# A transformer layer on one core: where a mixer slot puts its attention work, and which engine normalises group A's outputs

## The chip, the cores and the metric

One core of a Trainium2 chip runs one program. The metric is the device time of one execution in microseconds, median of three runs. The engines are named as in the profile: PE (TensorE, matmuls and transposes), PEld (its weight loads), DVE (VectorE), ACT (ScalarE), POOL (GpSimd), SP (SyncE, which only issues DMAs). Each runs its own list of instructions in order and waits on semaphores that the others raise.

## The reference

One layer of an encoder, for 512 prompt positions and, with a past of 512, for 32 sample positions. What matters here:

```
mod = silu(c) @ w_mod + b_mod             # shift, scale, gate for both sub-layers
h   = RMSNorm(x) * (1 + scale_a) + shift_a
z   = h @ w_in                            # q, k, v of groups A and B
A (8 heads, 128 wide): two softmax maps over two halves of q and k,
    w = p0 - lambda * p1;  o = w @ v
    o = RMSNorm(o over the 128) * g * (1 - lambda_init)      # g = subln_g, one value per column
B (16 heads, 64 wide): softmax with a sink over a window, o = p @ v
x = x + gate_a * (concat(A, B) @ w_out)
x = x + gate_f * (silu(conv(h2 @ w_up)) gated @ w_down)      # then a last RMSNorm
```

The normalisation of A multiplies each row (a position) by one number, 1/rms, and each column by one number, g. Once the 128 x 128 result is turned, a column of it is a partition.

## The kernel before

Positions stand on the free axis of the transposed activations: T = 544 columns in two halves of 272, D = 2048 in 16 k-tiles of 128. All large products are made of three matmuls per k-tile, high x high, low part of x, low part of w (`products`, L1590 to L1592). A weight chunk of 128 x 1024 is loaded by SP into one of four raw buffers, ACT copies its high part (w_hi, L829), DVE subtracts for the low part (w_lo, L1188).

**Half-steps and slots.** The projection z is computed slab by slab: 36 slabs of 128 columns, each in two half-steps (hf), 72 in all; one half-step takes 16 k-tiles, 48 matmuls. The attention is cut into points, `TURNS`: for each A head i = 0 to 3 for the four prompt blocks of 128 queries, i = 4 and 5 for the two softmax maps of the sample; for each B head pair four. The points of A head h are worked on in half-steps 6(h+1) to 6(h+1)+5, one to a half-step, while PE makes the slabs of the next head; so group A fills half-steps 6 to 53. B's points share half-steps in twos. `make_slots` gives the list of slots (half-step, part, parts, point t, item), and each engine's block walks that list in its own written order; nothing is planned at run time. In slot k, `pt` is the point of slot k-1 and `pp` that of slot k-2, where they have an output (i = 4 of A has none).

**A point's way.** Its score is made at the end of the slot before its own (`score`, L1645, into a PSUM bank). DVE adds the bias and takes the maximum (`softmax_max`, L1307, L1314), ACT the exponential with row sums (`softmax_exp`, L899), DVE joins the two maps (`combine`, L1334 to L1338). One slot later PE turns the probabilities (`turn_probs`, L1663, into bank 6), ACT (for A) or DVE (for B) copies them to SBUF (L919 to L922), PE multiplies by the values (`values`, L1679, into bank 7). For A, ACT then scales the result by 1/sum (o_raw, L951) and sums its squares (L952), POOL makes 1/rms in two small steps (`rstd`, L710, L711), and DVE multiplies o_raw by 1/rms and by g (o_norm, L1379; g was broadcast to all partitions, 128 x 128). Another slot later PE turns o_norm (`turn_output`, L1688) and ACT copies it into oT (L928).

**Beside it.** During half-steps 2 to 49 the parts of `mod` that are wanted later are computed off PE: SP loads 80 chunks of w_mod (L512), between the chunks of w_in (L520) and into the same four buffers. Half of each chunk's sum is made on DVE (`late_sum`, L1276, L1279), the other half as products on ACT (`late_mul`, L888) and sums on POOL (`late_add`, L725). `late_of` gives a slot's chunks: `begin` and `end`, one or none each, 1.67 per half-step on average. A raw buffer is free when DVE's w_lo has read it, or, for a chunk of w_mod, when DVE's late sum and ACT's late product have (`slot_free`, L489 to L493); SP issues strictly in stream order.

**The order around the change.** PE in a slot: quarter of the half-step's products, turn of the probabilities (pt), quarter, turn of the output (pp), quarter, values (pt), score of the next point, a turn of k or v (item), last quarter (`products_between`). ACT: exp (t), copy of the probabilities, copy of the output (pp), w_hi of the chunk two half-steps on, `late_mul` of begin, o_raw and square (pt), item, `late_mul` of end. DVE: z out of PSUM (L1289), copies for B, w_lo, combine (t), maximum of the next point, `late_sum` of begin, o_norm (pt), `late_sum` of end. POOL: `late_add` of begin, rstd (pt), table of the next head's bias, stores and loads of k and v, `late_add` of end. In the six slots of the tail (half-step None) PE puts the first tiles of the output projection in place of the products.

Of the kernel before, what the change touches and what calls it, by code (L numbers as in the profile page):

```python
# [33 lines left out]
ALU = mybir.AluOpType  # L34
ACT = mybir.ActivationFunctionType

P = 128
# [74 lines left out]
def is_a(t):  # L112
    return TURNS[t][0] < A_HEADS


def has_out(t):
    return not (is_a(t) and TURNS[t][1] == 4)
# [27 lines left out]
TAIL = len(SLOTS) - 6  # L145
# [58 lines left out]
def scored_ahead(t):  # L204

    return is_a(t) or TURNS[t][1] > 0
# [8 lines left out]
def prev_out(k, back):  # L215

    t = SLOTS[k - back][3] if k >= back else None
    return t if t is not None and has_out(t) else None
# [22 lines left out]
def late_of(hf, part, parts):  # L241

    if hf is None:
        return [], []
    c = [n for n, h in enumerate(LATE_AT) if h == hf]
    if parts == 1:
        return c[:1], c[1:]
    return (c[:1] if part == 0 else c[1:] if part == 1 else []), []
# [56 lines left out]
def build(nc, A, O):  # L305
# [5 lines left out]
    with ctx:  # L311
        def on(stack, name, shape, dt=F32):
            return stack.enter_context(nc.sbuf_tensor(name, shape, dt))
# [54 lines left out]
        tab_a = on(st1, "tab_a", [P, TAB])  # L368
        tab_b = on(st1, "tab_b", [P, 256])
        tab = [on(st1, f"tab{i}", [P, TAB]) for i in range(2)]  # L370
        gsub = on(st1, "gsub", [P, P])
        st1.close()

        st2 = ExitStack()
# [202 lines left out]
        def _(pool):  # L577
# [89 lines left out]
            for x in "kv":  # L667
# [4 lines left out]
            pool.wait_ge(scratch_out, 16 * 4)  # L672
            load_past("k", 0)
            load_past("v", 0)
            pool.dma_start(gsub[:, :], A["subln_g"].partition_broadcast(P).rearrange("p a n -> p (a n)")
                           ).then_inc(ld_sub, 16)

            step(pool.iota(tab_a[:, :], pattern=[[1, TAB]], base=-512, channel_multiplier=-1,
                           allow_small_or_imprecise_dtypes=True))
# [53 lines left out]
            for k, (hf, part, parts, t, item) in enumerate(SLOTS):  # L733
                pt = prev_out(k, 1)
                begin, end = late_of(hf, part, parts)
                for n in begin:
                    late_add(n)
                if pt is not None and is_a(pt):
                    rstd(pt)
                if t is not None and TURNS[t][1] == 0 and next_table < 16:  # L740
                    table(next_table)
                    next_table += 1
                if item:
                    natural(*item)
                    if item[1] == "p" and next_pk < 10:
                        load_past("k", next_pk)
                        next_pk += 1
                if pt is not None and TURNS[pt][1] == (5 if is_a(pt) else 3):
                    last_of_kv = pt + 1 == len(TURNS) or kv_of(TURNS[pt + 1][0]) != kv_of(TURNS[pt][0])
                    if last_of_kv and next_pv < 10:  # L750
                        pool.wait_ge(t_pv, OUT_COUNT[pt])
                        load_past("v", next_pv)
                        next_pv += 1
                for n in end:
                    late_add(n)
# [42 lines left out]
        def _(act):  # L798
# [111 lines left out]
            h_hi(KT - 1)  # L910
            for k, (hf, part, parts, t, item) in enumerate(SLOTS):
                pt, pp = prev_out(k, 1), prev_out(k, 2)
                if t is not None and scored_ahead(t):
                    softmax_exp(t)
                if pt is not None and is_a(pt):
                    act.wait_ge(b6_done, USE6[("p", pt)])
                    if pv_blocks(pt)[0][0] == P:
                        n = P * len(pv_blocks(pt)[0][3])
                        act.activation(probsT[:, 0:n], B6[:, 0:n], ACT.Copy).then_inc(b6_free, 1)  # L919
                    else:  # L920
                        act.activation(probsT[:, 0:P], B6[:, 0:P], ACT.Copy)
                        act.activation(probsT[0:TS, P:P + TS], B6[0:TS, P:P + TS], ACT.Copy).then_inc(b6_free, 1)  # L922
                if pp is not None:
                    act.wait_ge(t_ot, OUT_COUNT[pp])
                    if TURNS[pp][0] >= KT - 8:
                        act.wait_ge(m_late, LATE1 // LPG * LGT)
                    for n, c, tok, _b in pv_blocks(pp):
                        ins = act.activation(oT[:, TURNS[pp][0], tok:tok + n],  # L928
                                             B7[:, 256 + c:256 + c + n], ACT.Copy)
                    ins.then_inc(t_otev, 1)  # L930
                if t is not None and not scored_ahead(t):
                    softmax_exp(t)
                if hf is not None and part == 0 and hf + 2 < FC0:
                    hi_early(hf + 2)
                begin, end = late_of(hf, part, parts)
                for n in begin:
                    late_mul(n)
# [188 lines left out]
        def _(dve):  # L1126
# [214 lines left out]
            for k, (hf, part, parts, t, item) in enumerate(SLOTS):  # L1341
                pt = prev_out(k, 1)
                if (hf and part == 0) or k == TAIL:
                    z_out(hf - 1 if hf else ZH - 1)
                if hf == 5:
                    dve.wait_ge(ld_sub, 16)
                    dve.tensor_scalar(gsub[:, :], gsub[:, :], 1.0 - LAMBDA_INIT, None, ALU.mult).then_inc(small_ok, 1)
                    dve.wait_ge(small_ok, 1)
                if t is not None and not scored_ahead(t):
                    softmax_max(t)  # L1350
                if pt is not None and not is_a(pt):
                    dve.wait_ge(b6_done, USE6[("p", pt)])
                    if TURNS[pt][1] < 3:
                        dve.tensor_copy(probsT[:, :], B6[:, :]).then_inc(b6_free, 1)
                    else:
                        dve.tensor_copy(probsT[:, 0:2 * P], B6[:, 0:2 * P])
                        for e in range(2):
                            c = 256 + 64 * e
                            dve.tensor_copy(probsT[:, c:c + TS], B6[:, c:c + TS])
                            ins = dve.tensor_copy(probsT[0:TS, c + TS:c + 2 * TS], B6[0:TS, c + TS:c + 2 * TS])  # L1360
                        ins.then_inc(b6_free, 1)
                if hf is not None and part == 0 and hf + 2 < FC0:
                    lo_early(hf + 2)
                if hf is None:
                    for kt in TAIL_SPLITS[k - TAIL]:
                        dve.wait_ge(n_hi, KT + kt + 1)
                        dve.tensor_tensor(x_lo[:, kt, :], oT[:, kt, :], x_hi[:, kt, :].bitcast(F32), ALU.subtract
                                          ).then_inc(x_ok, 1)
                if t is not None and has_out(t):
                    combine(t)  # L1370
                if next_ahead(k) is not None:
                    softmax_max(next_ahead(k))
                begin, end = late_of(hf, part, parts)
                for n in begin:
                    late_sum(n)
                if pt is not None and is_a(pt):
                    dve.wait_ge(t_rstd, OUT_A[pt])
                    n = pv_blocks(pt)[0][0]
                    dve.scalar_tensor_tensor(out=o_norm[0:n, 0:P], in0=o_raw[0:n, :], scalar=stats[0:n, pt % 4, 19:20],  # L1379
                                             in1=gsub[0:n, :], op0=ALU.mult, op1=ALU.mult).then_inc(t_on_a, 1)  # L1380
                for n in end:
                    late_sum(n)

            def gated(n, h, b, gate):

# [139 lines left out]
        def _(pe):  # L1525
# [183 lines left out]
            for k, (hf, part, parts, t, item) in enumerate(SLOTS):  # L1709
                pt, pp = prev_out(k, 1), prev_out(k, 2)  # L1710
                n = KT // parts
                cut = [n * part + n * c // 4 for c in range(5)]

                def products_between(c):


                    if hf is not None:
                        tiles(hf, range(cut[c], cut[c + 1]))
                    elif k > TAIL and c in (1, 2):
                        tiles(ZH + c - 1, TAIL_SPLITS[k - TAIL - 1])  # L1720

                if t is not None and not scored_ahead(t):
                    score(t)
                products_between(0)
                if pt is not None:
                    turn_probs(pt)
                products_between(1)
                if pp is not None:
                    turn_output(pp)
                products_between(2)  # L1730
                if pt is not None:
                    values(pt)
                if next_ahead(k) is not None:
                    score(next_ahead(k))
                if item:
                    kv_item(*item)
                products_between(3)
            tiles(ZH, TAIL_SPLITS[-1])
            tiles(ZH + 1, TAIL_SPLITS[-1])
            for hf in range(ZH + 2, ZH + OH):  # L1740
# [118 lines left out]
```

## Time and profile before

| | us |
|---|---|
| median of 3 runs (lowest, highest) | 2827.66 (2827.05, 2828.97) |
| the profiled execution | 2829.49 |
| its span in the profile | 2827.7 |
| PE busy in it | 2620.3 (93%) |
| DVE, ACT, POOL busy | 1658.2, 994.1, 638.3 |

A stretch of the span is read with the busy time of each engine in it and with the clock that was granted to PE, as a share of 2.4 GHz. A wait is idle time of an engine right before an instruction, put down to what was signalled last. The mixer's half-steps run from about 182 us to 950 us of the span; the stretch 231 to 734 holds half-steps 6 to 53.

### The profile page before, as it was taken

To read this page: it belongs to the slowest core of one execution; us is meant where nothing else is said; L and a number is where in the kernel's file an instruction comes from. 1 tells how busy PE (TensorE), PEld (TensorE's weight loads), DVE (VectorE), ACT (ScalarE), POOL (GpSimd) and SP (SyncE) were. 2 spreads that over 40 slices of the span, in tenths; PEclk is the share of its full clock that TensorE was granted. 3 is DMA by queue.
4 is the path that set the end of the run, shared out by engine and by line. 5 is a ranking of instruction groups with operands and counts; after the bars stand their busy time and mean duration, and the time that the engine had idled before them with its cause. 6 is when DMAs were issued, how large, how long until landed. Compare 5 with 4: busy or idle time off the path is not lost.

```text
span 2827.7 us, 50285 instructions
## 1 busy us (share of the span) xinstructions
PE 2620.3 (93%) x19815; PEld 2469.0 (87%) x19815; DVE 1658.2 (59%) x2930; ACT 994.1 (35%) x1975; POOL 638.3 (23%) x534
## 2 busy tenths in 40 slices
PE   6688888888999999789999999999999999999997
PEld 2267777777898899689999999999999999999997
DVE  6878777776445788785444444444444444444454
ACT  5555554554434433542222222222222222222224
POOL 4776566665100344331000000000000000000003
PEclk9889999999999999899999999999999999999998
DMA  9764444445221556253233333223333222322231
GB/s 299 229 196 147 157 137 155 148 146 144 61 63 47 154 165 174 74 157 110 83 89 90 91 90 90 87 80 90 90 90 91 86 83 87 91 85 84 87 105 67
DMA packets 416207, 325.00 MB, mean 115 GB/s; under 512 B 44394, under 2 KB 360202, under 8 KB 414880
## 3 DMA queue, kind: packets, MB, share of 16 engines
q1 hardware_dynamic: 410032, 302.55, 35.9%
q0 software_dynamic: 5248, 14.63, 1.6%
q10 hardware_dynamic: 688, 4.47, 0.4%
q8 instruction: 169, 2.77, 0.4%
q14 instruction: 70, 0.57, 0.1%
HBM read 307.73 MB, written 14.07 MB: 114 GB/s over the span
## 4 chain that ended last, share of the span: by engine, by line
PE 55%; DVE 5%; DMA 2%; issue 2%; ACT 1%; SPq 1%; ACTq 0%; POOL 0%; DVEq 0%
PE ps L1592 18%; PE ps L1590 18%; PE ps L1591 18%; DVE late_f L1279 3%; DMA w_raw<-in_w_out 2%; ACT w_hi L829 1%; SPq L538 1%; DVE w_lo L1188 0%; DVE x L1387 0%; DVE x_lo L1180 0%; ACT x_hi L1022 0%; DVE cv L1173 0%; PE ps L1809 0%; DVE late_f L1276 0%; DMA w_raw<-in_w_up 0%
## 5 line engine op out<-in xcount | busy, mean ns | idle before, releaser
L1590 PE MATMUL ps<-x_hi,w_hi 128*128 128x272 f32 x4480 | 1328.2, 296 | 44.7 <-DVE w_lo L1188 26.0
L1592 PE MATMUL ps<-x_hi,w_lo 128*128 128x272 f32 x4480 | 1308.2, 292 | 0.0
L1591 PE MATMUL ps<-x_lo,w_hi 128*128 128x272 f32 x4480 | 1298.0, 290 | 0.0
L1590 PEld LDWEIGHTS ps<-x_hi,w_hi 128*128 128x128 f32 x4480 | 855.1, 191 | 62.4 <-issue 23.8
L1591 PEld LDWEIGHTS ps<-x_lo,w_hi 128*128 128x128 f32 x4480 | 856.4, 191 | 0.0
L1592 PEld LDWEIGHTS ps<-x_hi,w_lo 128*128 128x128 f32 x4480 | 853.6, 191 | 0.0
L1188 DVE TENSOR_TENSOR w_lo<-w_raw,w_hi 128x1024 fp32r<-128x1024 f32 x432 | 536.5, 1270 | 463.8 <-ACT w_hi L829 462.7
L829 ACT ACTIVATE w_hi<-w_raw 128x1024 fp32r<-128x1024 f32 x432 | 442.0, 1056 | 837.2 <-PE ps L1592 545.3
L1591 PE MATMUL ps<-y_lo,w_hi 128*128 128x272 f32 x1408 | 407.3, 289 | 0.0
L1590 PE MATMUL ps<-y_hi,w_hi 128*128 128x272 f32 x1408 | 405.7, 288 | 0.0
L1592 PE MATMUL ps<-y_hi,w_lo 128*128 128x272 f32 x1408 | 405.0, 288 | 0.0
L784 POOL TENSOR_TENSOR ext<-cv 128x544 f32<-128x544 f32 x1 | 1.5, 1512 | 1473.4 <-ACT cv L1085 1473.4
L1590 PEld LDWEIGHTS ps<-y_hi,w_hi 128*128 128x128 f32 x1408 | 265.5, 189 | 0.1
L1592 PEld LDWEIGHTS ps<-y_hi,w_lo 128*128 128x128 f32 x1408 | 264.8, 188 | 0.0
L1591 PEld LDWEIGHTS ps<-y_lo,w_hi 128*128 128x128 f32 x1408 | 264.6, 188 | 0.0
L1387 DVE SCALAR_TENSOR_TENSOR x<-ps,mod,x 128x272 f32<-128x272 f32 (+2 forms) x576 | 207.8, 400 | 95.6 <-PE ps L1592 95.5
L1035 ACT ACTIVATE ext<-ps 128x272 f32<-128x272 f32 (+2 forms) x264 | 73.9, 317 | 528.5 <-PE ps L1592 528.0
L725 POOL TENSOR_TENSOR oT<-oT 128x512 f32<-128x512 f32 x150 | 216.3, 1442 | 180.3 <-ACT oT L888 169.5
L1431 DVE COPY ext<-cols 128x2 f32 (+1 forms) x88 | 14.9, 169 | 400.8 <-ACT ext L1035 400.8
L725 POOL TENSOR_TENSOR late_f<-late_f 128x512 f32<-128x512 f32 x90 | 138.4, 1537 | 146.6 <-ACT late_f L888 137.8
L1279 DVE SCALAR_TENSOR_TENSOR oT<-w_raw,cs,oT 128x512 f32<-128x512 f32 x150 | 162.8, 1085 | 3.7
L1279 DVE SCALAR_TENSOR_TENSOR late_f<-w_raw,cs,late_f 128x512 f32<-128x512 f32 x90 | 129.4, 1437 | 3.1
(200 smaller groups left out, 2221.8 us busy)
## 6 DMA issues: line engine op xcount, KB each, us to landing
w_raw<-in_w_mod SPq DMA_DIRECT2D x192, 512.0 KB, 4.7
w_raw<-in_w_up SPq DMA_DIRECT2D x176, 512.0 KB, 4.7
w_raw<-in_w_down SPq DMA_DIRECT2D x88, 512.0 KB, 4.4
w_raw<-in_w_in SPq DMA_DIRECT2D x56, 512.0 KB, 3.9
w_raw<-in_w_in SPq DMA_DIRECT2D x32, 256.0 KB, 3.7
w_raw<-in_w_out SPq DMA_DIRECT2D x16, 512.0 KB, 5.3
w_raw<-in_w_out SPq DMA_DIRECT2D x64, 128.0 KB, 3.9
x_transposed<-xT SPq DMA_DIRECT2D x4, 1088.0 KB, 5.7
```

What stands on the lines that cost most here:

```text
L538: sp.dma_start(dst[64 * u:64 * u + 64, 4 * m:4 * m + 4, :], src.rearrange("(i p) n -> p i n", p=64)).then_inc(ld_raw[slot], 16)
L725: ins = pool.tensor_tensor(acc, late_prod(n, 0) if p == 0 and k == 1 else acc, late_prod(n, k), ALU.add)
L784: pool.tensor_tensor(f_sum, f_sq[0][:, 0:T], f_sq[1][:, 0:T], ALU.add).then_inc(f_add, 1)
L829: act.activation(w_hi[c % NW][:, :], w_raw[raw][:, :], ACT.Copy).then_inc(s_hi, 1)
L1035: ins = act.activation(ext[x][:, a + 2 + 2 * g:a + 2 + 2 * g + n], bank(2 * x + h)[:, a - HALF[h][0]:a - HALF[h][0] + n], ACT.Copy)
L1188: dve.tensor_tensor(w_lo[c % NW][:, :], w_raw[raw][:, :], w_hi[c % NW][:, :].bitcast(F32), ALU.subtract).then_inc(s_lo, 1)
L1279: ins = dve.scalar_tensor_tensor(out=acc_d(g), in0=w, scalar=c, in1=acc_d(g), op0=ALU.mult, op1=ALU.add)
L1387: ins = dve.scalar_tensor_tensor(out=x1[:, n, a:a + m], in0=b[:, a - HALF[h][0]:a - HALF[h][0] + m], scalar=mod[:, gate + n, g:g + 1], in1 ...
L1431: dve.tensor_copy(ext[x][:, TP + 2:TP + 4], cols[:, STATE:STATE + 2, bass.ds(tile, 1)] .rearrange("p a b -> p (a b)")).then_inc(ext_ok, 1)
L1590: pe.matmul(out[:, 0:n], hi_w, hi_x, start=first, stop=False)
L1591: pe.matmul(out[:, 0:n], hi_w, lo_x, start=False, stop=False)
L1592: return pe.matmul(out[:, 0:n], lo_w, hi_x, start=False, stop=last)
```

## The change

PE has two attention points in a slot: products (5 of 16 k-tiles), then the turns of the probabilities (pt) and of the output (pp) together, products (7), then values, score and item, products (4). A's o_norm is made by ACT with 1/rms alone, at the head of its next slot; g is one column, loaded as such, and goes in as the scale of ACT's copy of the turned output. ACT's w_hi now stands ahead of that copy. On DVE the first late sum goes to the head of the slot, combine ahead of w_lo, the maximum of the next point to the end. On POOL rstd goes ahead of the first late add.

```diff
-        gsub = on(st1, "gsub", [P, P])
+        gsub = on(st1, "gsub", [P, 1])
# POOL
-            pool.dma_start(gsub[:, :], A["subln_g"].partition_broadcast(P).rearrange("p a n -> p (a n)")
-                           ).then_inc(ld_sub, 16)
+            pool.dma_start(gsub[:, :], A["subln_g"].rearrange("a p -> p a")).then_inc(ld_sub, 16)
...
+                if pt is not None and is_a(pt):
+                    rstd(pt)
                 for n in begin:
                     late_add(n)
-                if pt is not None and is_a(pt):
-                    rstd(pt)
# ACT
                 pt, pp = prev_out(k, 1), prev_out(k, 2)
+                if pp is not None and is_a(pp):
+                    act.wait_ge(t_rstd, OUT_A[pp])
+                    n = pv_blocks(pp)[0][0]
+                    act.activation(o_norm[0:n, 0:P], o_raw[0:n, :], ACT.Copy, scale=stats[0:n, pp % 4, 19:20]
+                                   ).then_inc(t_on_a, 1)
                 if t is not None and scored_ahead(t):
                     softmax_exp(t)
...
+                if hf is not None and part == 0 and hf + 2 < FC0:
+                    hi_early(hf + 2)
                 if pp is not None:
                     act.wait_ge(t_ot, OUT_COUNT[pp])
...
+                    if is_a(pp):
+                        act.wait_ge(small_ok, 1)
                     for n, c, tok, _b in pv_blocks(pp):
-                        ins = act.activation(oT[:, TURNS[pp][0], tok:tok + n],
-                                             B7[:, 256 + c:256 + c + n], ACT.Copy)
+                        ins = act.activation(oT[:, TURNS[pp][0], tok:tok + n], B7[:, 256 + c:256 + c + n], ACT.Copy,
+                                             scale=gsub[:, 0:1] if is_a(pp) else 1.0)
                     ins.then_inc(t_otev, 1)
                 if t is not None and not scored_ahead(t):
                     softmax_exp(t)
-                if hf is not None and part == 0 and hf + 2 < FC0:
-                    hi_early(hf + 2)
# DVE
+                begin, end = late_of(hf, part, parts)
+                for n in begin:
+                    late_sum(n)
                 if pt is not None and not is_a(pt):
...
+                if t is not None and has_out(t):
+                    combine(t)
                 if hf is not None and part == 0 and hf + 2 < FC0:
                     lo_early(hf + 2)
...
-                if t is not None and has_out(t):
-                    combine(t)
+                for n in end:
+                    late_sum(n)
                 if next_ahead(k) is not None:
                     softmax_max(next_ahead(k))
-                begin, end = late_of(hf, part, parts)
-                for n in begin:
-                    late_sum(n)
-                if pt is not None and is_a(pt):
-                    dve.wait_ge(t_rstd, OUT_A[pt])
-                    n = pv_blocks(pt)[0][0]
-                    dve.scalar_tensor_tensor(out=o_norm[0:n, 0:P], in0=o_raw[0:n, :], scalar=stats[0:n, pt % 4, 19:20],
-                                             in1=gsub[0:n, :], op0=ALU.mult, op1=ALU.mult).then_inc(t_on_a, 1)
-                for n in end:
-                    late_sum(n)
# PE
-                cut = [n * part + n * c // 4 for c in range(5)]
+                cut = [n * part + n * c // 12 for c in (0, 4, 9, 12)]
...
-                    elif k > TAIL and c in (1, 2):
+                    elif k > TAIL and c:
                         tiles(ZH + c - 1, TAIL_SPLITS[k - TAIL - 1])
...
                 products_between(0)
                 if pt is not None:
                     turn_probs(pt)
-                products_between(1)
                 if pp is not None:
                     turn_output(pp)
-                products_between(2)
+                products_between(1)
                 if pt is not None:
                     values(pt)
...
-                products_between(3)
+                products_between(2)
```

## Rows read from the trace of the kernel before

**Rows 1.** Stretches: us, busy (instructions) of PE, PEld, DVE, ACT, POOL; PEclk, DMA, GB/s.
```profile
231.00:734.00 503.00, 435.86 (x3102) 386.51 (x3101) 369.87 (x683) 250.44 (x595) 291.60 (x271) 0.95 0.46 143
734.00:905.00 171.00, 166.97 (x1325) 150.79 (x1325) 79.51 (x303) 69.02 (x241) 16.41 (x23) 1.00 0.22 56
905.00:950.00 45.00, 39.95 (x294) 34.66 (x293) 28.44 (x90) 27.50 (x83) 4.83 (x6) 0.92 0.25 81
```

**Rows 2.** Waits from 231 to 734: who for whom, us in total, times, longest.
```profile
DVE w_lo L1188 <- ACT w_hi L829: 99.1, 43, 5.2
...
PE ps L1688 <- DVE o_norm L1379: 53.7, 30, 3.0
...
PE ps L1663 <- DVE scores L1338: 11.8, 10, 2.9
```

**Rows 3.** Waits of SP's DMA queue from 231 to 734.
```profile
SPq L520 <- DVE oT L1279: 178.9, 41, 6.8
```

**Rows 4.** Timeline 512.2 to 526.5, one slot: start, us, engine, what, idle before.
```profile
512.35 0.83 PE L1679 MATMUL ps<-v_nat,probsT 128*128 128x128 f32 x6
...
513.42 1.06 ACT L829 ACTIVATE w_hi<-w_raw 128x1024 fp32r<-128x1024 f32 x1 [2.10 <-DMA w_raw<-in_w_in]
...
515.61 0.34 ACT L951 ACTIVATE o_raw<-ps,stats 128x128 f32<-128x128 f32 x1
...
515.78 2.99 POOL L725 TENSOR_TENSOR oT<-oT 128x512 f32<-128x512 f32 x2 [5.32 <-ACT oT L888]
...
516.11 0.19 ACT L952 ACTIVATION_READ_ACCUMULATOR square<-ps,stats 128x1 f32 x1
...
516.68 1.33 ACT L888 ACTIVATE oT<-w_raw,cs 128x512 f32<-128x512 f32 x2
...
517.67 0.65 PE L1663 MATMUL ps<-ident,scores 128*128 128x128 f32 x4
...
518.58 1.54 DVE L1279 SCALAR_TENSOR_TENSOR oT<-w_raw,cs,oT 128x512 f32<-128x512 f32 x2
...
518.85 0.53 POOL L710 TENSOR_SCALAR stats<-stats 128x1 f32<-128x1 f32 x1
...
519.04 0.29 PE L1591 MATMUL ps<-x_lo,w_hi 128*128 128x272 f32 x1
...
519.41 0.28 PE L1591 MATMUL ps<-x_lo,w_hi 128*128 128x272 f32 x1
...
519.47 1.08 POOL L711 TENSOR_TENSOR stats<-stats,tiny 128x1 f32<-128x1 f32 x1
...
520.15 0.37 SPq L520 DMA_DIRECT2D w_raw<-in_w_in  x1
520.50 0.84 POOL L650 DMA_DIRECT2D out_ak_p<-k_nat  x1
...
520.58 2.22 DVE L1379 SCALAR_TENSOR_TENSOR o_norm<-o_raw,stats,gsub 128x128 f32<-128x128 f32 x1 [0.46 <-POOL stats L711]
...
522.85 0.40 PE L1688 MATMUL ps<-ident,o_norm 128*128 128x128 f32 x1 [3.03 <-DVE o_norm L1379]
...
523.28 0.43 PE L1591 MATMUL ps<-x_lo,w_hi 128*128 128x272 f32 x1
...
523.96 0.43 PE L1591 MATMUL ps<-x_lo,w_hi 128*128 128x272 f32 x1
...
524.38 1.06 ACT L829 ACTIVATE w_hi<-w_raw 128x1024 fp32r<-128x1024 f32 x1 [0.82 <-DMA w_raw<-in_w_in]
```

**Rows 5.** Groups by shape from 231 to 734: busy us, mean ns, idle before.
```profile
L1379 DVE SCALAR_TENSOR_TENSOR o_norm<-o_raw,stats,gsub 128x128 f32<-128x128 f32 x32 | 26.5, 828 | 7.9 <-POOL stats L711 7.9
...
L725 POOL TENSOR_TENSOR oT<-oT 128x512 f32<-128x512 f32 x134 | 191.2, 1427 | 171.7 <-ACT oT L888 162.0 <-issue 2.3 <-POOL oT L725 0.3
...
L696 POOL TENSOR_SCALAR tab<-tab_a 128x640 f32<-128x640 f32 x6 | 13.1, 2180 | 0.3
...
L928 ACT ACTIVATE oT<-ps 128x128 f32<-128x128 f32 x32 | 8.9, 277 | 82.1 <-PE ps L1688 82.1
```

More of the change, by code:

```diff
@@ L1347, in _ @@
                     dve.tensor_scalar(gsub[:, :], gsub[:, :], 1.0 - LAMBDA_INIT, None, ALU.mult).then_inc(small_ok, 1)
-                    dve.wait_ge(small_ok, 1)
                 if t is not None and not scored_ahead(t):
                     softmax_max(t)
+                begin, end = late_of(hf, part, parts)
+                for n in begin:
+                    late_sum(n)
                 if pt is not None and not is_a(pt):
```

## The prediction, made before the changed kernel was run

> **What bounds the kernel now.** I read the stretches first, then the waits of PE inside one stretch, then SP's waits, then one slot in order of time, and last the groups with their means.
>
> The stretches [rows 1] cut the mixer in three. While group B's points run (734 to 905) PE is busy 166.97 of 171.00 us at clock 1.00: nothing is to be had there. While group A's points run (231 to 734, half-steps 6 to 53, so 48 slots of 10.5 us) PE is busy 435.86 of 503.00 us, so 67 us idle, and its mean granted clock is 0.95. The tail (905 to 950) has 5 us of idle time.
>
> The waits of that stretch [rows 2] say what the 67 us are: 53.7 us are the turn of the output (L1688) behind DVE's o_norm, 30 times, up to 3.0 us; 11.8 us are the turn of the probabilities (L1663) behind DVE's combine. That is 65.5 of 67.
>
> Why o_norm is late can be read in one slot [rows 4]. PE ends the values of a point at 513.18 (512.35 + 0.83). ACT reads them only at 515.61, because it stands in its order behind w_hi, whose chunk landed at 513.42, and a mod product. Pool then takes its late add (515.78, 2.99 us) before the two small rstd steps (518.85 to 520.55). DVE does o_norm from 520.58, for 2.22 us, and PE, which had nothing left since 519.82 (3.03 before), turns the output at 522.85. From the end of the values to the turn: 9.7 us. The chunk of 513.42 was itself late: SP's longest wait of this kind [rows 3] is the issue of w_in behind DVE's late sum, 178.9 us in 41 times, and in rows 4 a late sum of 518.58 to 520.12 is followed by the issue at 520.15. So DVE's old order closes a ring: late sum, load, w_hi, w_lo, combine, max, late sum. That ring is also behind the 99.1 us for which DVE's w_lo waits for w_hi [rows 2].
>
> The stall has a second price, the clock. One k-tile of products (three matmuls) goes from 519.04 to 519.41, 0.37 us, ahead of the stall, and from 523.28 to 523.96, 0.68 us, right behind it [rows 4]: the lower of the two levels, 1.2 instead of 2.4 GHz. A mean of 0.95 over 503 us means 50 us at the lower level. There PE does 0.37/0.68 = 0.54 of its work, a loss of 23 us if it was busy throughout; it was busy for 87% (435.86/503), so 20 us.
>
> **The change part by part.**
>
> *The normalisation.* DVE loses 32 operations of 828 ns and 8 smaller ones, some 30 us of its 369.87 [rows 5, 1]. ACT gets 40 activations of 128x128 from SBUF with a scale from memory. None such is in the trace. The nearest below is the copy of the output, 0.28 us with a constant scale [rows 5]; above it the 128x512 products, 0.67 each (1.33 for two, 516.68 in rows 4). I take o_raw's 0.34 us (515.61), which has the same size and the same kind of scale: 14 us on an engine busy for 250 of 503 [rows 1], 11 to 27 by the two ends. The same o_norm on DVE took 2.22 us in rows 4 and 0.83 in the mean. The Trainium skill (SBUF — State Buffer, "Who interferes with whom") says that a VectorE instruction with two SBUF inputs contends with a GpSimd one that reads SBUF, while ScalarE never waits for anyone; the trace agrees on the DVE side, and by the rule ACT's price would stay at its lowest.
>
> *Pool's order.* rstd now goes before the slot's late add: the 2.99 us between 515.78 and 518.85 leave the path. The price: the late add waits for o_raw, which in rows 4 would move it by 0.5 + 1.7 us. ACT's next product but one waits for it, a slot later, so this hides under a slot.
>
> *DVE's order.* The first late sum goes to the head of the slot, before combine and w_lo. It needs only its own chunk, which was issued a slot earlier, so the ring above opens: the next w_in chunk no longer hangs on combine and max. What then releases it is ACT's mod product in the middle of the slot; a load takes 4.2 us (issued 520.15, w_hi at 524.38) and so ends near the start of the next slot, where w_hi wants it some 3 us in. Were it late still, w_hi's wait would stay: rival B. combine comes out ahead of w_lo and needs only ACT's exp; its reader on PE is five k-tiles into the next slot. I cost the 11.8 us of L1663 as gone.
>
> *PE's two points.* Of 16 k-tiles, 5, 7 and 4 stand before the turns, between turns and values, and after the score (before: 4, 4, 4, 4). Between the values and the turn of that point's output stood 12 k-tiles, now 9: 9 x 0.37 = 3.3 us, with the turn of the probabilities (0.65) 4.0 us, score and kv item not counted. The new chain in that time: o_raw to the end of the square's sum 0.7 us (515.61 to 516.30), rstd 1.7, o_norm 0.34: 2.8 us; ACT's own queue behind o_raw ends at 518.01, 2.4 us after o_raw began, as rstd would. Slack 1.2 us. The added wait stands at the head of ACT's slot, and exp, the copy of the probabilities, w_hi and the copy of the output stand behind it; all but exp are wanted later than o_norm itself.
>
> *What is late next.* Pool. In the slot that also builds the table (once a head) it has rstd 1.7, two late adds of two 1.427 us steps (5.7), the table 2.18 and two DMA issues of 0.84: 11.3 us [rows 4, 5], where the slot should now be (503 - 85.5)/48 = 8.7 us. It falls 2.6 us behind; 1.2 of that is slack, the other 1.4 reach PE, with a little left for the slot after: I take 1.6 us a head, 13 us for eight. Bounds: 0, and 40 turns x 1.0 us.
>
> *Small edits at no price.* g as one column: its load is issued ahead of the first point and waited for once, by DVE in half-step 5 (uncovered, at most the 4.2 us of a whole chunk); on the copy of the output the scale costs at most 0.08 us x 40 on ACT, hidden. w_hi before that copy delays it by 1.06 us at most, and the values that need it stand 7 k-tiles (2.6 us) behind. In B's slots and in the tail the products only change places: PE has no idle time in B, and the tail can give between 4 us gain (of its 5) and 2 us loss (the last turn has nothing in front of it); I take 0.
>
> *Sum.* 53.7 + 11.8 + 20 = 85.5 gained, 13 lost again: 72.5. Against the profiled execution's own 2829.49: 2757. That one lies 1.8 us above the median shown, so against 2827.66: 2755. In sentences of its own: the Trainium skill (TensorE: Matmul & The Clock Gate, "Terms") prices throttled time at that time x (1 - K/N), which for 50 us at half is 25 us where I have 20; by it the sum would be 5 us better, 2750.
>
> **The rivals.**
>
> *A. The wait only changes its releaser.* turn_output now stands before 11 of 16 k-tiles and the values, so ACT behind Pool may be late as DVE was. For it: Pool is busy 291.6 of 503 us, 70% of the shorter stretch, and in order. Against it: 2.8 us of chain in 4.0. Price: half of the 53.7 stays (27) and the clock goes on falling (20): gain 38, 2790.
>
> *B. DVE takes over.* If w_hi goes on landing late, DVE keeps its 99.1 us of waiting beside 340 us of work: 439 us where PE would need 418. The gain is 64, less the 13: 51, 2777. For it: DVE then is at 81% without any wait. Against it: its waits move off the ring.
>
> *C. Slower: a ring through Pool.* Place: rstd behind both late adds of the slot before. Loop: 7 k-tiles 2.6, values 0.83, o_raw and square 0.7, two late adds 5.7, rstd 1.7, o_norm 0.34, turn 0.4 = 12.3 us, against 10.5 now. If it closes in the two of three slots with two mod chunks: 32 x 1.8 = 58 lost, 16 x 1.8 = 29 gained, 2857. It decides from 3.9 us of Pool work in front of rstd in the mean. Against it: Pool's 291.6/48 = 6.1 us a slot.
>
> *D. Nothing to measure*, gains and new waits equal.
>
> **How the numbers follow.** Forecast 0.61 (its own range 2738 to 2772: all of 85.5 and the tail's 4, or twice the new wait and a little), A 0.20, B 0.10, C 0.06, D 0.03. A difference under 0.2% (5.7 us) can't be told from none. Faster 0.91, the same 0.03, slower 0.06. The range goes from 2738 to past A's time, 2795; outside it lie C, D, the worse part of A and a little below.
>
> **What would show it.** Right: between half-steps 6 and 53 PE's waits at the output's turn fall from 53.7 to under 15 us, those at the probabilities' turn to under 3, the mean clock there to 0.99 or more, the stretch shrinks from 503 to about 430 us, DVE's wait for w_hi to under half of 99, B's stretch stays 171. Wrong: PE's turn waits for ACT's o_norm over 25 us and that for Pool's rstd (A, C); or PE idles behind DVE's combine or zq, with w_hi still behind its load (B).

## The result, and the profile after

The changed kernel takes 2740.2 us (2738.19 to 2740.53) where the kernel before, on the same chip, takes 2828.31: a ratio of 0.9679 (95% interval 0.9665 to 0.9694), which on the 2827.66 us shown ahead is 2736.9 us, 91 us less. Measured once more among the experiments the ratio was 0.9711 (0.9698 to 0.9724), 82 us less. So the change is faster, by more than the 72.5 us of the sum, and the first measurement lies just past the fast end of the range. Differences below some 0.3% between separate measurements are therefore read from stretches of the traces here, not from times.

The stretches of the changed kernel, cut where DVE takes half-steps 0, 6, 53 and 71 out of PSUM (columns as in rows 1), and then the same first two stretches of the kernel before. The second of them is called the middle stretch from here on.

```profile
183.40:227.10 43.70, 42.17 (x333) 41.13 (x331) 39.29 (x46) 19.21 (x29) 37.41 (x26) 1.00 0.65 193
227.10:638.20 411.10, 404.53 (x3061) 366.71 (x3061) 350.50 (x631) 262.80 (x628) 295.13 (x272) 1.00 0.58 173
638.20:824.50 186.30, 182.56 (x1451) 164.68 (x1450) 86.35 (x332) 78.21 (x270) 17.30 (x25) 1.00 0.21 54
```
```profile
182.20:231.40 49.20, 45.80 (x346) 44.09 (x345) 38.21 (x47) 20.34 (x34) 39.05 (x28) 0.97 0.51 159
231.40:726.90 495.50, 428.84 (x3050) 380.91 (x3048) 365.77 (x670) 247.18 (x584) 290.98 (x269) 0.95 0.46 144
```

DVE takes half-step 6 out late. Counted by PE's own products, 48 to a half-step, PE has by then done 85% of half-step 7 in the kernel before and 75% in the changed one. So the middle stretch lacks A's first two half-steps, 6 and 7, nearly whole, and so does the stretch 231 to 734, which was said ahead to hold half-steps 6 to 53. PE's own half-steps 6 to 53, from the first product of half-step 6 to the first of half-step 54, are these, before and after:

```profile
213.40:728.02 514.62, 444.90 (x3161) 395.41 (x3159) 382.29 (x695) 255.93 (x602) 304.01 (x278) 0.95 0.46 145
```
```profile
213.49:639.37 425.88, 417.25 (x3160) 378.33 (x3158) 364.30 (x654) 267.93 (x639) 304.36 (x277) 1.00 0.58 173
```

They went from 514.6 to 425.9 us, 88.7 of the 88.9 by which the profiled span fell (2827.7 to 2738.8). PE's idle time there went from 69.7 to 8.6 us, and its busy time, for the same instructions, from 444.9 to 417.3: most of that is the clock, 0.95 before and 1.00 now. The middle stretch, by which the experiments are compared, went from 495.5 to 411.1 us, 84.4 us less, PE's idle time in it from 66.7 to 6.6. Half-steps 0 to 5 gave 1.1 us (40.3 to 39.2 by PE's products). B's stretch is what it was (187.6 before, 186.3 now).

The waits of the changed kernel from 227.1 to 638.2 answer to rows 2, SP's own from 227 to 638 to rows 3:

```profile
POOL stats L709 <- ACT square L958: 75.9, 28, 7.3
...
ACT o_norm L915 <- POOL stats L710: 33.8, 15, 4.2
...
DVE w_lo L1194 <- ACT w_hi L828: 12.8, 8, 4.2
...
PE ps L1688 <- ACT o_norm L915: 5.1, 5, 1.5
...
PE ps L1679 <- ACT probsT L923: 1.9, 1, 1.9
```
```profile
SPq L493 <- ACT oT L887: 273.3, 65, 8.2
...
SPq L520 <- DVE oT L1285: 1.6, 3, 0.8
```

At the turn of the output PE waits 5.1 us in place of 53.7, at that of the probabilities not at all; the 1.9 us are one wait of the values for the copy of the probabilities. DVE waits 12.8 us for w_hi in place of some 99. SP no longer waits for DVE's late sum before it loads w_in (1.6 in place of 178.9): ACT's mod product now comes last, as forecast.

The slot that answers to rows 4 (same kind of point):

```profile
511.71 0.83 PE L1679 MATMUL ps<-v_nat,probsT 128*128 128x128 f32 x6
...
512.58 0.37 ACT L957 ACTIVATE o_raw<-ps,stats 128x128 f32<-128x128 f32 x1 [0.50 <-PE ps L1679]
...
513.38 0.95 POOL L709 TENSOR_SCALAR stats<-stats 128x1 f32<-128x1 f32 x1 [0.79 <-ACT square L958]
...
514.41 0.95 POOL L710 TENSOR_TENSOR stats<-stats,tiny 128x1 f32<-128x1 f32 x1
...
515.92 0.39 ACT L915 ACTIVATE o_norm<-o_raw,stats 128x128 f32<-128x128 f32 x1
516.09 0.37 SPq L520 DMA_DIRECT2D w_raw<-in_w_in  x1
...
517.81 0.27 PE L1688 MATMUL ps<-ident,o_norm 128*128 128x128 f32 x1
...
518.51 1.05 ACT L828 ACTIVATE w_hi<-w_raw 128x1024 fp32r<-128x1024 f32 x1
```

ACT stands ready when PE ends the values (it waits 0.50 us for them; before it came 2.4 us late). From the values' end to o_norm's end it is 3.8 us (512.54 to 516.31), and PE, which came to the turn on its own at 517.81, had 1.5 us to spare. w_hi at 518.51 has no wait for its load.

### The profile page after: what moved, and what is told of

Read it like the earlier page. It is cut to its first block, busy times and chain, and to the rows that moved or that the text cites. A ratio compares the mean times of both kernels' runs of the same rounds, so it can differ in the third digit from the quotient of the medians.

```text
span 2738.8 us, 50324 instructions
## 1 busy us (share of the span) xinstructions
PE 2592.2 (95%) x19815; PEld 2452.4 (90%) x19815; DVE 1641.2 (60%) x2890; ACT 1010.4 (37%) x2015; POOL 643.4 (23%) x534
## 4 chain that ended last, share of the span: by engine, by line
PE 77%; DVE 8%; POOL 4%; issue 4%; DMA 3%; ACT 2%; SPq 1%; ACTq 0%; POOLq 0%; DVEq 0%
PE ps L1590 24%; PE ps L1592 23%; PE ps L1591 23%; DVE late_f L1285 3%; PE ps L1679 2%; PE ps L1645 2%; DMA w_raw<-in_w_out 2%; DMA w_raw<-in_w_mod 1%; POOL oT L724 1%; POOL xT L622 1%; ACT w_hi L828 1%; DVE w_lo L1194 1%; POOL xT L627 1%; DVE oT L1285 1%; PE ps L1663 1%
## 5 line engine op out<-in xcount | busy, mean ns | idle before, releaser
L1194 DVE TENSOR_TENSOR w_lo<-w_raw,w_hi 128x1024 fp32r<-128x1024 f32 x432 | 546.3, 1292 | 346.8 <-ACT w_hi L828 345.8
L724 POOL TENSOR_TENSOR oT<-oT 128x512 f32<-128x512 f32 x150 | 224.3, 1495 | 31.7 <-ACT oT L887 23.8
L1285 DVE SCALAR_TENSOR_TENSOR oT<-w_raw,cs,oT 128x512 f32<-128x512 f32 x150 | 179.3, 1195 | 2.8
```

Of the source, the lines that this page charges most:

```text
L724: ins = pool.tensor_tensor(acc, late_prod(n, 0) if p == 0 and k == 1 else acc, late_prod(n, k), ALU.add)
L1194: dve.tensor_tensor(w_lo[c % NW][:, :], w_raw[raw][:, :], w_hi[c % NW][:, :].bitcast(F32), ALU.subtract).then_inc(s_lo, 1)
L1285: ins = dve.scalar_tensor_tensor(out=acc_d(g), in0=w, scalar=c, in1=acc_d(g), op0=ALU.mult, op1=ALU.add)
```

## The experiments

Two theories. R: what bounded the A stretch was the ring late sum, load, w_hi, w_lo, combine, max, late sum, and o_norm was only where it came out. N: what counted was o_norm's own late start, behind Pool's add and in DVE's queue. All lengths are of the middle stretch (us), read like the rows above. They are good to some 4 us, because DVE's cut meets PE at a different point of half-step 7 in each kernel:

| kernel | stretch | PE idle | clock | ratio to before (95%) |
|---|---|---|---|---|
| before | 495.5 | 66.7 | 0.95 | 1 |
| e6: before, o_norm on ACT | 491.0 | 63.7 | 0.95 | 0.9991 (0.9982 to 1.0001) |
| e5: before, DVE's new order | 437.6 | 24.2 | 0.98 | 0.9790 (0.9766 to 0.9814) |
| changed | 411.1 | 6.6 | 1.00 | 0.9679 (0.9665 to 0.9694) |
| e1: changed, Pool's old order | 424.7 | 15.6 | 0.99 | 0.9742 (0.9714 to 0.9770) |
| e2: changed, three points | 412.2 | 5.5 | 0.99 | 0.9699 (0.9669 to 0.9729) |
| e4: changed, w_hi's old place | 410.7 | 6.8 | 1.00 | 0.9692 (0.9662 to 0.9721) |
| e10: changed, combine's old place | 413.5 | 7.0 | 0.99 | 0.9717 (0.9702 to 0.9732) |
| e11: changed, late sums' old place | 485.4 | 48.9 | 0.93 | 0.9971 (0.9959 to 0.9984) |
| e3: changed, DVE's old order | 507.3 | 65.1 | 0.91 | 1.0030 (1.0014 to 1.0046) |
| e9: e3, and w_hi's old place | 464.2 | 44.9 | 0.97 | 0.9904 (0.9882 to 0.9926) |
| e7: changed, table three times | 434.8 | 21.8 | 0.97 | 0.9768 (0.9745 to 0.9791) |
| e8: changed, table in the slot of i = 5 | 405.5 | 2.7 | 1.00 | 0.9693 (0.9680 to 0.9707) |

**e1, Pool's old order.**

```diff
-                if pt is not None and is_a(pt):
-                    rstd(pt)
                 for n in begin:
                     late_add(n)
+                if pt is not None and is_a(pt):
+                    rstd(pt)
```


> The changed kernel with Pool's old order: the late add of begin ahead of rstd. Theory R (the ring late sum, load, w_hi, w_lo, combine, max, late sum bounded the A stretch, and o_norm was only where it came out): the chain from the values to o_norm gets some 2.9 us longer, the slack swallows most of it, 2740 to 2750. Theory N (what counted was o_norm's own late start behind Pool and DVE): the 2.9 us come back on most of 40 turns, 40 to 80 us, 2780 to 2820, with PE's wait at the output's turn over 30 us.

2755.2 us, between the two and nearer the first: the stretch grows by 13.6 us, and PE's wait at the output's turn is 13.8 us in 10 times. The 2.9 us of the add reach PE in a quarter of the turns.

```profile
ACT o_norm L915 <- POOL stats L710: 72.7, 29, 5.2
...
PE ps L1688 <- ACT o_norm L915: 13.8, 10, 2.5
```

**e2, three points.**

```diff
-                cut = [n * part + n * c // 12 for c in (0, 4, 9, 12)]
+                cut = [n * part + n * c // 4 for c in range(5)]
...
                     turn_probs(pt)
+                products_between(1)
                 if pp is not None:
                     turn_output(pp)
-                products_between(1)
+                products_between(2)
```


> The changed kernel with PE's three attention points (4, 4, 4, 4 k-tiles) as before. Both theories give the two points no gain of their own: with 12 k-tiles instead of 9 in front of the output's turn its wait falls from 5.1 us to under 3, 2735 to 2742. If two points are worth something by themselves, 2755 or more.

As expected, the wait at the turn falls (0.3 us), but the values then wait 3.7 us for the copy of the output, and the stretch is the same. PE's two points, the first edit in the account of the change, are worth nothing beside the rest; alone in the kernel before they were not run.

**e3, DVE's old order, and e9, that with w_hi's old place** (e9 is e3 with the edit of e4, shown below).

```diff
 # e3
-                begin, end = late_of(hf, part, parts)
-                for n in begin:
-                    late_sum(n)
                 if pt is not None and not is_a(pt):
...
-                if t is not None and has_out(t):
-                    combine(t)
                 if hf is not None and part == 0 and hf + 2 < FC0:
                     lo_early(hf + 2)
...
-                for n in end:
-                    late_sum(n)
+                if t is not None and has_out(t):
+                    combine(t)
                 if next_ahead(k) is not None:
                     softmax_max(next_ahead(k))
+                begin, end = late_of(hf, part, parts)
+                for n in begin + end:
+                    late_sum(n)
```


> The changed kernel with DVE's old order (w_lo, combine, max, then both late sums); o_norm stays on ACT. Theory R: the ring is closed again, DVE's wait for w_hi goes from 13 back to some 90 us and 50 us or more come back, 2790 to 2820, the clock falls again. Theory N: under 15 us, 2740 to 2755.

> DVE's old order and ACT's old place of w_hi in the changed kernel together (o_norm on ACT, Pool's new order and PE's two points stay). With DVE's old order alone PE waited 62.5 us for the copy of the output, which on ACT stood behind w_hi and its late load. If that is why it was slower than the kernel before, putting w_hi behind the copy takes these waits away: 2790 to 2820. If the closed ring sets the slot whatever stands where, the waits turn up elsewhere: 2825 to 2840.

DVE's order alone, put back, closes the ring again and takes back more than all: 2838.6 us, 0.3% slower than the kernel before, and more than was expected. Waits of e3 from 232.4 to 739.7:

```profile
DVE w_lo L1194 <- ACT w_hi L828: 95.1, 39, 5.7
...
PE ps L1677 <- ACT oT L936: 62.5, 20, 4.8
```

and of e9 from 229.6 to 693.8:

```profile
DVE w_lo L1194 <- ACT w_hi L828: 88.5, 39, 4.5
...
PE ps L1686 <- ACT o_norm L915: 23.8, 20, 4.3
PE ps L1661 <- DVE scores L1344: 18.7, 11, 2.8
```

With the load late, ACT stands in w_hi, and what is queued behind it, the copy of the output, holds PE's values (L1677 there). With w_hi behind that copy the 62.5 us are gone, 43.1 us come off the stretch, and the shorter waits turn up at the two turns. So w_hi's new place is free when the ring is open (e4) and costs 43 us when it is closed. The ring is not the whole of it: e9 differs from e6 by Pool's order and PE's points, and is 26.8 us shorter; which of the two gives it while the ring is closed was not run.

**e4, w_hi's old place.** w_hi (`hi_early`) back behind the copy of the output.

```diff
-                if hf is not None and part == 0 and hf + 2 < FC0:
-                    hi_early(hf + 2)
                 if pp is not None:
...
+                if hf is not None and part == 0 and hf + 2 < FC0:
+                    hi_early(hf + 2)
                 begin, end = late_of(hf, part, parts)
```


> The changed kernel with ACT's w_hi in its old place, behind the copy of the output. Theory R: w_hi is some 0.5 us later, its buffers are freed a little later, under 5 us, 2738 to 2745. Rival: w_hi at once is what opens the ring on ACT's side, 10 us or more, 2750 to 2775.

No difference; the rival falls.

**e5, DVE's new order alone in the kernel before** (o_norm, still on DVE, goes last).

```diff
+                begin, end = late_of(hf, part, parts)
+                for n in begin:
+                    late_sum(n)
                 if pt is not None and not is_a(pt):
...
+                if t is not None and has_out(t):
+                    combine(t)
                 if hf is not None and part == 0 and hf + 2 < FC0:
                     lo_early(hf + 2)
...
-                if t is not None and has_out(t):
-                    combine(t)
+                for n in end:
+                    late_sum(n)
                 if next_ahead(k) is not None:
                     softmax_max(next_ahead(k))
-                begin, end = late_of(hf, part, parts)
-                for n in begin:
-                    late_sum(n)
                 if pt is not None and is_a(pt):
                     dve.wait_ge(t_rstd, OUT_A[pt])
...
-                for n in end:
-                    late_sum(n)
```


> The kernel before with DVE's new order alone: late sum of begin at the head, combine ahead of w_lo, late sum of end, maximum, and o_norm (still on DVE, with g) last. Theory R: the ring opens, most of the gain comes from this alone although o_norm stands behind the maximum: 2760 to 2790, DVE's wait for w_hi under 50 us. Theory N: o_norm is as late as before or later, 2815 to 2840.

Theory R: 57.9 of the 84.4 us, with o_norm later in DVE's order than it was. Waits from 226.1 to 663.7:

```profile
PE ps L1688 <- DVE o_norm L1381: 22.4, 17, 2.8
...
DVE w_lo L1188 <- ACT w_hi L829: 16.3, 8, 5.1
```

Of the other 26.5 us, between e5 and the changed kernel, Pool's order is worth 13.6 (e1). The rest is left to o_norm's move to ACT with the ring open by difference only; that was not run by itself.

**e6, o_norm on ACT alone in the kernel before** (g as one column goes with it, on the copy of the turned output).

```diff
+                if pp is not None and is_a(pp):
+                    act.wait_ge(t_rstd, OUT_A[pp])
+                    n = pv_blocks(pp)[0][0]
+                    act.activation(o_norm[0:n, 0:P], o_raw[0:n, :], ACT.Copy, scale=stats[0:n, pp % 4, 19:20]
+                                   ).then_inc(t_on_a, 1)
...
-                    dve.scalar_tensor_tensor(out=o_norm[0:n, 0:P], in0=o_raw[0:n, :], scalar=stats[0:n, pt % 4, 19:20],
-                                             in1=gsub[0:n, :], op0=ALU.mult, op1=ALU.mult).then_inc(t_on_a, 1)
```


> The kernel before with o_norm on ACT alone (at the head of its next slot, g on the copy of the turned output); the orders of DVE, Pool, w_hi and PE as before. Theory R: the ring stays closed, gain under 20 us, 2808 to 2830. Theory N: most of the gain, 2745 to 2780.

Theory N falls: no difference in time that is clear of noise, 4.5 us in the stretch. Waits from 232 to 723: the name of the wait changes, the sum hardly (62.2 for 65.5 us).

```profile
ACT o_norm L915 <- POOL stats L710: 96.5, 35, 5.3
...
PE ps L1688 <- ACT o_norm L915: 39.0, 23, 4.3
PE ps L1663 <- DVE scores L1344: 23.2, 18, 2.7
```

**e10 and e11, the two halves of DVE's order.**

```diff
 # e10
+                if hf is not None and part == 0 and hf + 2 < FC0:
+                    lo_early(hf + 2)
                 if t is not None and has_out(t):
                     combine(t)
-                if hf is not None and part == 0 and hf + 2 < FC0:
-                    lo_early(hf + 2)
 # e11
-                begin, end = late_of(hf, part, parts)
-                for n in begin:
-                    late_sum(n)
...
-                for n in end:
-                    late_sum(n)
                 if next_ahead(k) is not None:
                     softmax_max(next_ahead(k))
+                begin, end = late_of(hf, part, parts)
+                for n in begin + end:
+                    late_sum(n)
```


> The changed kernel with combine behind w_lo again, the late sum of begin still first. If the late sum's place alone opens the ring: 2738 to 2746. If combine ahead of w_lo is part of it: 2755 or more, with PE waiting at the probabilities' turn (L1663) again for 8 us or more.

> The changed kernel with both late sums behind the maximum again, combine still ahead of w_lo. If the late sum's place closes the ring: 2800 to 2840, with DVE's wait for w_hi at 80 us or more. If combine's place did it: 2740 to 2760.

It is the late sums' place: put back, it costs 74.3 us (e11), combine's 2.4 (e10). In e11 SP waits for the late sum again (from 227 to 640):

```profile
SPq L520 <- DVE oT L1285: 154.7, 40, 5.8
```

The 74.3 us are not the ring's price alone. As in e3, PE pays much of it at the values, behind a copy of the output that stands behind w_hi (from 229.9 to 715.3):

```profile
PE ps L1677 <- ACT oT L936: 46.5, 19, 4.0
```

With w_hi behind that copy, DVE's order as a whole is worth 53.5 us in the changed kernel (e9 against e4) and 57.9 in the kernel before (e5); e11 with w_hi's old place was not run. DVE's wait for w_hi in e11 is 43.8 us, not the 80 expected, and 95.1 in e3, which differs by combine's place alone: combine stands in that time and hides part of it. So combine's place, worth 2.4 us while the ring is open, is worth 21.9 once it is closed (e3 against e11).

**e7, Pool's table three times**, for the step of the sum that came out wrong.

```diff
+                    for _ in range(2):
+                        step(pool.tensor_scalar(tab[qi % 2][:, :], tab_a[:, :], slope_a(qi), None, ALU.mult))
                     pool.tensor_scalar(tab[qi % 2][:, :], tab_a[:, :], slope_a(qi), None, ALU.mult
                                        ).then_inc(tab_ok, 1)
```


> The changed kernel with each A head's bias table built three times on Pool (two of them for nothing): 2 x 2.2 us more Pool work once a head, 35 us in all. By the step of the prediction that took Pool's lateness to reach PE beyond 1.2 us of slack, nearly all of it comes through: 2765 to 2775, with PE's wait at the output's turn at 30 us or more. Rival: Pool stands idle ahead of rstd for 75.9 us in 28 of 40 turns, so it is not late to begin with, and under a third comes through: 2740 to 2752.

2765.0 us, between the two: of some 33 us added (16 operations of 2.04 us in the mean; 13 of them, 26.5 us, in this stretch) 23.7 come through there, and PE's wait at the output's turn is 20.2 us in 7 times (from 228.9 to 663.7), of 4.4 us at the longest, the rest being clock.

```profile
PE ps L1690 <- ACT o_norm L917: 20.2, 7, 4.4
```

So Pool's lateness in that slot does reach PE; the prediction had the mechanism and the place.

**e8, the table where Pool has no rstd,** beside the changed kernel itself.

```diff
+                if t is not None and is_a(t) and TURNS[t][1] == 5:
+                    table(next_table)
+                    next_table += 1
                 if pt is not None and is_a(pt):
                     rstd(pt)
                 for n in begin:
                     late_add(n)
-                if t is not None and TURNS[t][1] == 0 and next_table < 16:
+                if t is not None and not is_a(t) and TURNS[t][1] == 0 and next_table < 16:
```


> The changed kernel with A's next bias table built by Pool in the slot of point i = 5, where no rstd is asked of it, instead of the slot of i = 0. In the changed kernel PE's five waits at the output's turn (5.1 us) all belong to points i = 0, whose rstd stands behind the late add and the table of the slot before by 3.0 to 3.6 us. If this lateness is what is left of the price of the new wait: those waits fall under 1 us, 3 to 6 us faster than the changed kernel beside it, 2733 to 2738. Rival (PE only loses the same time elsewhere, DVE or ACT being next): within 2 us of it.

> The changed kernel as it is, beside the one with the table moved: 2738 to 2742 whatever the theory.

2738.4 against 2744.0 us (2 us more than was expected of the changed kernel), measured side by side; their intervals (0.9680 to 0.9707, 0.9698 to 0.9724) just overlap, so by time it is not settled. The traces are clearer: no wait at the output's turn is left, PE is idle for 2.7 us, and the stretch is 405.5 against 410.2 us (the changed kernel beside it) and 411.1.

```profile
229.30:634.80 405.50, 402.78 (x3061) 365.29 (x3061) 357.93 (x631) 263.20 (x628) 293.51 (x271) 1.00 0.59 175
```
```profile
225.60:635.80 410.20, 403.65 (x3061) 365.20 (x3061) 350.78 (x632) 262.36 (x628) 296.94 (x272) 1.00 0.58 174
```

## Why the prediction was right or wrong, point by point

The direction, the place and the mechanism held: the ring through the raw buffers (e3, e5, e11), its outlet at the output's turn, the clock as its second price, and none of the rivals A to D. The size was short by 16.4 us of the span. By PE's own half-steps 6 to 53 the terms are:

| term | forecast | measured |
|---|---|---|
| PE's idle time | -65.5 + 13 = -52.5 | 69.7 to 8.6: -61.1 |
| its busy time, forecast as the clock | -20 | 444.9 to 417.3: -27.6 |
| the rest of the span | 0 | -0.2 |
| sum | -72.5 | -88.9 |

Two steps failed in size: the price of the new wait at the output's turn and the price of the clock. The fast end of the range, 89.5 us of gain, allowed for no new wait at all and for 4 us from the tail, but left the clock's 20 us no room. The first measurement lies about 1 us past it, less than the width of its interval (2733 to 2741 us), and the second lies inside: on which side of the end a measurement falls is chance, the two short terms are not.

*"I take 1.6 us a head, 13 us for eight."* This step failed in size: 5.1 us, in five of the eight turns, stand where it put 13. Here is the slot it meant, in the changed kernel: rstd of a point i = 0, behind the add that came after the table.

```profile
387.89 0.38 PE L1679 MATMUL ps<-v_nat,probsT 128*128 128x128 f32 x2
...
388.83 0.20 ACT L958 ACTIVATION_READ_ACCUMULATOR square<-ps,stats 128x1 f32 x1
...
389.08 3.47 POOL L724 TENSOR_TENSOR oT<-oT 128x512 f32<-128x512 f32 x2
...
392.64 0.24 POOL L709 TENSOR_SCALAR stats<-stats 128x1 f32<-128x1 f32 x1
...
392.96 1.09 POOL L710 TENSOR_TENSOR stats<-stats,tiny 128x1 f32<-128x1 f32 x1
...
394.08 0.40 ACT L915 ACTIVATE o_norm<-o_raw,stats 128x128 f32<-128x128 f32 x1 [4.18 <-POOL stats L710]
...
394.54 0.33 PE L1688 MATMUL ps<-ident,o_norm 128*128 128x128 f32 x1 [1.50 <-ACT o_norm L915]
```

Pool is 3.6 us late, more than the 2.6 worked out, and ACT waits 4.2 us; PE loses 1.5 of it. What was wrong is the slack: I had put 1.2 us and left the score and the kv item out of it "not counted", though they stand on PE between the values and the turn. PE had work there for 4.8 us (the values end at 388.27, it stood idle from 393.04), not 4.0, and for 5.3 in the slot shown first. Elsewhere Pool stands ready (75.9 us of waiting in 28 turns). e7 shows that the path is there, e8 that its 5 us can be had back.

*"It was busy for 87%, so 20 us."* This step failed in size, too: PE's busy time fell by 27.6 us. The factor was the wrong one. Read in steps of half a microsecond from 231 to 734, the clock is low in 14 places, and PE is busy for 51.6 of the 54.0 us of these steps: 96%, against 87% over the whole stretch. But that is the smaller part of the error, for the 50 us were rounded up: 1 less the clock adds up to 23.9 us there, which at half speed is 47.8 us, and with the right factor the step gives 21 us (47.8 x 0.46 x 0.96). In PE's own half-steps 6 to 53, 1 less the clock adds up to 25.6 us before and to 1.7 after, so at most 23.9 of the 27.6 us are the clock. The other 4 us show even where the clock reads 1.00 in both kernels: in half-step 9 PE is busy for 9.06 us before and for 8.87 after. What makes them is open.

The Trainium skill's formula (TensorE: Matmul & The Clock Gate, "Terms"), which I had set beside it at 25 us, gives 23.9 us by these sums, nearer to the 27.6 than my 20. It has no term for idle time inside the low stretches, and there it gives too much: for e3, where PE was busy for 86.7 of 94.5 us of such steps, 42.7 us over the changed kernel's middle stretch where PE's busy time is 37.7 longer, for e11 34.1 where it is 32.0.

*The stretch* was wrongly named. From 231 on it lacks most of A's half-steps 6 and 7, where PE waits another 2.6 us for DVE to take z out (at 221.26) and the clock falls once more. With other waits of 1.6 us that makes the 4.2 us of idle time that the sum left out; afterwards 3.5 us stand beside the 5.1 at the output's turn. Half-steps 0 to 5, also left out, gave 1.1 us: they take 40.3 us wherever the late sums stand behind the maximum (before, e3, e6, e9, e11) and 39.2 where they stand first (e5, e1, changed).

*Right:* L1663's 11.8 us went, though not because combine moved (e10 has none of them either): it was the ring as well. DVE's wait for w_hi fell to 12.8. ACT's price was 0.40 us an o_norm (forecast 0.34) and stays hidden. Pool's old order costs 13.6 us (e1), which the prediction had only as a share of 53.7. *Half right:* DVE was to lose 30 us of work and lost 15.3 (365.8 to 350.5), because much of what stays there takes longer (by groups, the late sums 143.5 to 156.2 us, the small step behind the maximum 9.4 to 21.5, w_lo 61.8 to 69.0), while combine takes less (45.9 to 28.6). *Not shown by itself:* the load of g as one column.

## What to carry to other kernels

The engine on which a wait is booked is not always where it is made: follow the buffer that the late instruction reads back through its load to whoever freed it, and if that closes on the same slot, open the ring at its cheapest place, here by moving the one operation that frees the buffer to the head of its engine's list. An instruction moved ahead of others in an engine's list is free only as long as its input is early; the same move cost 43 us where it was late. Count every instruction that stands between two ends when you work out slack, and weigh the clock's price by how busy the engine is while the clock is low (96% here), not by its share of the whole stretch (87%). A stretch cut by one engine's instructions can miss work of another: count the other's own instructions.

## What the runs showed that was not expected

DVE's w_lo, with two inputs in SBUF, takes longer in the changed kernel. Its groups by line before (231 to 734), after (227.1 to 638.2) and in e8 (229.3 to 634.8):

```profile
L1188 DVE TENSOR_TENSOR w_lo<-w_raw,w_hi 128x1024 fp32r<-128x1024 f32 x48 | 61.8, 1287 | 99.1 <-ACT w_hi L829 99.1
```
```profile
L1194 DVE TENSOR_TENSOR w_lo<-w_raw,w_hi 128x1024 fp32r<-128x1024 f32 x47 | 69.0, 1469 | 12.8 <-ACT w_hi L828 12.8
```
```profile
L1197 DVE TENSOR_TENSOR w_lo<-w_raw,w_hi 128x1024 fp32r<-128x1024 f32 x47 | 60.4, 1285 | 11.7 <-ACT w_hi L831 11.6
```

1287 to 1469 ns for the same shape. Read one by one, 35 of the 47 after take 1.20 to 1.29 us, and the other 12 take 1.66 to 2.67. Every one of the 12 overlaps a late add of Pool; before, it was 4 of 48, and those overlap one too. (Some that overlap one stay short.) It is not that the schedule is denser: e8's middle stretch is shorter yet, and there 5 of 47 are long. Seven of the 12 come once a head, close behind the table, and moving the table took all but one of them away. So the long ones go with meeting Pool's adds, and where Pool's work lies in the slot sets how many of them meet.

o_norm on ACT had a mean of 396 ns with Pool as busy as ever, where DVE's was 828. That agrees with the rule of the Trainium skill (SBUF — State Buffer, "Who interferes with whom") weighed in the prediction. What the runs add is that moving one operation of Pool changes how many such pairs meet. For w_lo they come to some 8 us of DVE time in the changed kernel, for which PE has no wait in the trace.
